# Six small moves in a three-layer transformer kernel bound by TensorE: casts, a weight's low half, a gelu table, gates, final gains and two convolution taps

## The reference

```python
def first_block(x, c, ctx, c_ctx, ...):            # DEPTH = 2 layers
    for l in range(DEPTH):
        with_ctx = l < DEPTH - 1                   # layer 0 also updates ctx
        u = x * (1.0 + sc1) + sh1                  # modulated by c; uc likewise
        y, yc = token_mixer(u, uc, rope, w_in[l], ...)
        x = layer_norm(alpha * x + g1 * y, ln1_g[l], ln1_b[l])
        x = layer_norm(alpha * x + g2 * sq_relu_mlp(x * (1.0 + sc2) + sh2, w1[l], ...), ...)

def token_mixer(...):
    a, qkv, o_pre, g_if, cq, ckv, kr, gates = split(u @ w_in + b_in)
    y_conv = conformer_conv(a, ...)       # h = val * sigmoid(gate); 31 taps by token; norm; product
    h_x = mlstm_bidir(q_x, k_x, v_x, ...) # chunks of 128 tokens, 4 heads, both directions
    o_x = mla_blockwise(...)              # low-rank queries and keys, 8 heads, softmax
    return gated_merge(gates, y_conv, y_ml, o_x @ w_mla_out, w_out, b_out)

def gated_merge(gates, y_a, y_b, y_c, w_out, b_out):
    g_a, g_b, g_c = split(sigmoid(gates))
    return (g_a * y_a + g_b * y_b + g_c * y_c) @ w_out + b_out
```

## Time and profile before

| | |
|---|---|
| median of 3 runs | 3194.83 us (3194.47 to 3195.56) |
| profiled execution, its own time | 3197.05 us |
| its span, first to last instruction | 3194.6 us |
| mean granted clock of TensorE | 0.997 |
| PE busy | 3147.1 us |
| DVE busy | 1995.1 us |
| ACT busy | 1223.0 us |
| POOL busy | 1207.0 us |

### The profile page before, as it was taken

How to read it: one execution, slowest core, us unless ns; L and a number is a source line. 1 busy time by engine, 2 the same in 40 slices (tenths; PEclk the granted TensorE clock), 3 DMA queues, 4 the chain that set the end, 5 groups by cost and what they waited for, 6 DMA issues and landing times. The chain is left out here.

```text
span 3194.6 us, 46651 instructions
## 1 busy us (share of the span) xinstructions
PE 3147.1 (99%) x17058; PEld 2549.9 (80%) x17058; DVE 1995.1 (62%) x2910; ACT 1223.0 (38%) x1744; POOL 1207.0 (38%) x610
## 2 busy tenths in 40 slices
PE   8999999999999999999999999999999999999998
PEld 7888557888888888887776477778988877788887
DVE  6958476448876423146997673678533676777626
ACT  3232345522244323133542555245333375322223
POOL 3332066233333232323441463544444324444443
PEclk9999999999999999999999999999999999999999
DMA  6222130235412222222222103663333232233333
GB/s 232 58 60 53 42 88 21 56 106 160 146 58 66 63 62 64 60 65 69 78 80 51 26 1 110 209 188 90 93 92 93 83 105 60 86 92 92 96 96 106
DMA packets 470029, 275.94 MB, mean 86 GB/s; under 512 B 53985, under 2 KB 453857, under 8 KB 468706
## 3 DMA queue, kind: packets, MB, share of 16 engines
q1 hardware_dynamic: 469714, 273.55, 29.1%
q10 hardware_dynamic: 144, 0.02, 0.0%
HBM read 269.31 MB, written 4.19 MB: 86 GB/s over the span
## 5 line engine op out<-in xcount | busy, mean ns | idle before, releaser
L386 POOL TENSOR_TENSOR weights_low<-weight_ring,weights_high 128x1024 fp32r<-128x1024 f32 (+1 forms) x399 | 970.5, 2434 | 1675.7 <-ACT weights_high L377 1660.6
L377 ACT ACTIVATE weights_high<-weight_ring 128x1024 fp32r<-128x1024 f32 (+1 forms) x408 | 410.2, 1006 | 1033.0 <-PE ps L487 991.9
L482 PE MATMUL ps<-features_high,weights_high 128*128 128x512 f32 (+2 forms) x1792 | 605.8, 353 | 4.2 <-DVE features_low L2904 2.4
L483 PE MATMUL ps<-features_low,weights_high 128*128 128x512 f32 (+2 forms) x1792 | 602.3, 353 | 0.0
L482 PEld LDWEIGHTS ps<-features_high,weights_high 128*128 128x128 f32 (+1 forms) x1792 | 336.9, 188 | 62.0 <-DVE features_low L3851 4.1
L483 PEld LDWEIGHTS ps<-features_low,weights_high 128*128 128x128 f32 (+1 forms) x1792 | 336.6, 188 | 51.6
L482 PE MATMUL ps<-u_high,weights_high 128*128 128x512 f32 (+2 forms) x944 | 364.7, 390 | 5.4 <-DVE u_low L4197 2.7
L487 PE MATMUL ps<-features_high,weights_low 128*128 128x512 f32 (+2 forms) x1792 | 365.9, 351 | 0.0
L483 PE MATMUL ps<-u_low,weights_high 128*128 128x512 f32 (+2 forms) x944 | 359.1, 385 | 0.0
L487 PEld LDWEIGHTS ps<-features_high,weights_low 128*128 128x128 f32 (+1 forms) x1792 | 288.9, 188 | 44.7
L1349 DVE SCALAR_TENSOR_TENSOR conv<-conv,vectors 128x512 f32<-128x512 f32 (+1 forms) x480 | 306.5, 708 | 1.2 <-DVE conv L1257 1.0
(11 more groups left out here) (665 smaller groups left out, 5290.2 us busy)
## 6 DMA issues: line engine op xcount, KB each, us to landing
weight_ring<-in_w SPq DMA_DIRECT2D x256, 256.0 KB, 3.0
weight_ring<-in_w_in SPq DMA_DIRECT2D x246, 256.0 KB, 3.2
conv<-in_w_mod_columns SPq DMA_DIRECT2D x64, 512.0 KB, 4.6
weight_ring<-in_w_up SPq DMA_DIRECT2D x88, 256.0 KB, 3.1
weight_ring<-in_w_out SPq DMA_DIRECT2D x48, 256.0 KB, 3.1
weight_ring<-in_w_mod SPq DMA_DIRECT2D x32, 256.0 KB, 3.5
weight_ring<-in_w_down SPq DMA_DIRECT2D x32, 256.0 KB, 3.0
first_modulation<-in_first_modulation SPq DMA_DIRECT2D x4, 1024.0 KB, 9.5
```

The costliest lines, as they stand in the source:

```text
L377: act.activation(core.ring_high[:, split_slot(run, q), 0:n], core.ring[:, slot, 0:n], ACT.Copy).then_inc(core.high_ready.sem, 1)
L386: pool.tensor_tensor(core.ring_low[:, split_slot(run, q), 0:n], core.ring[:, (run.first + q) % SLOTS, 0:n], high.bitcast(F32), ALU.subtrac ...
L482: pe.matmul(to, w_high[:, k, 0:m], high(k, a, b), start=(first and k == ks[0]), stop=False, skip_group_check=True)
L483: pe.matmul(to, w_high[:, k, 0:m], low(k, a, b), start=False, stop=False, skip_group_check=True)
```

## The change

Six places in the order of work, no new computation:

- Convolution of layer 1: `cuts` from (1, 11, 14, 17) to (1, 9, 12, 15). Two taps fewer stand before the first of the three later inputs, the distances between the inputs stay, two more taps follow the last.
- Layer 0's casts for the mLSTM stage move from behind step 1 to behind step 5, after the last turned key of the loop.
- Layer 1's first low half of the output weights is made by DVE inside the merge (after the first sum of the last pair) and no longer by POOL; POOL waits for all eight split tiles before it goes on with group 1.
- Mixer stage, DVE: gate 0's product stands ahead of the token scales, tiles 0 and 1 are split before gate 1's product.
- Mixer stage, ACT: an activation of one column loads gelu's table right after the square root; tile 0, gate 1 and tile 1 come before the second weight group's high half.
- Embedding stage, ACT: the final gains of tiles 4 and 5 stand before the last two sigmoids instead of behind them.

```diff
--- before.py
+++ after.py
@@ -1359,7 +1359,7 @@
                 nc.vector.tensor_scalar(conv[:, f, a:b], pads[:, f, at:at + b - a], w_dw[:, 0, f:f + 1],
                                         col(core, f"b_dw{l}", f), ALU.mult, ALU.add).then_inc(conv_step.sem, 1)
             if f == 0:
-                cuts = (1, 11, 21, CONV_K) if seam is None else (1, 11, 14, 17)
+                cuts = (1, 11, 21, CONV_K) if seam is None else (1, 9, 12, 15)
                 for q in range(1, 4):
                     taps(0, cuts[q - 1], cuts[q])
                     conv_input(q)
@@ -2231,7 +2231,7 @@
                     turning.clear_maxima()
                 if i in turn_at:
                     turning.copy_keys(dve, i - 1)
-                if i == turn_at[0]:
+                if i == (turn_at[-1] + 1 if both else turn_at[0]):
                     turning.round_triangles()
                     turning.round_ones(dve)
         dve.wait_ge(s["scored"].sem, s["scored"].at(2 * len(steps_of)))
@@ -2944,6 +2944,9 @@
                         nc.vector.tensor_tensor(m, m, prod[:, f, 0:w], ALU.add).then_inc(merged_step.sem, 1)
                         if (b, i) != (1, 3):
                             late.make(dve, b, i, f)
+                    if not both and last and b == 2 and f == 0:
+                        dve.wait_ge(core.split_ready.sem, split_count(run, 3, 3))
+                        low_part(core, dve, run_out, 0, 0)
                 if b == 0 and isinstance(i, int) and i == 0:
                     norm.scale(dve)
             if b == 0:
@@ -3570,7 +3573,12 @@
 
     @block.gpsimd
     def _(pool):
-        low_parts(core, pool, run_out, run)
+        if not both:
+            pool.wait_ge(merged_split.sem, merged_split.at(KT))
+            pool.wait_ge(core.split_ready.sem, split_count(run_out, 0, 0))
+        for g in range(0 if both else 1, run_out.groups):
+            low_part(core, pool, run_out, g // run_out.body, g % run_out.body)
+        low_parts(core, pool, run)
 
     @block.tensor
     def _(pe):
@@ -4186,6 +4194,12 @@
         nc.vector.tensor_tensor(mix[:, 0], misc, u[:, 0], ALU.mult).then_inc(gmlp_done.sem, 1)
         dve.wait_ge(mixed.sem, mixed.at(2))
         nc.vector.tensor_tensor(mix[:, 1], misc, u[:, 1], ALU.mult).then_inc(gmlp_done.sem, 1)
+
+        def gate_conv(f):
+            dve.wait_ge(gb_ready.sem, gb_ready.at(f + 1))
+            nc.vector.tensor_tensor(xc[:, f], xc[:, f], gb[:, f], ALU.mult).then_inc(xc_gated.sem, 1)
+
+        gate_conv(0)
         dve.wait_ge(std.sem, std.at(1))
         link(nc.vector.reciprocal(token_std, token_std))
         mark("token scales")
@@ -4197,12 +4211,9 @@
             nc.vector.tensor_tensor(split.low[:, k, :], mix[:, k], split.high[:, k, :].bitcast(F32), ALU.subtract)\
                 .then_inc(mix_split.sem, 1)
 
-        for k in (6, 7):
+        for k in (6, 7, 0, 1):
             split_mix(k)
-        for f in range(2):
-            dve.wait_ge(gb_ready.sem, gb_ready.at(f + 1))
-            nc.vector.tensor_tensor(xc[:, f], xc[:, f], gb[:, f], ALU.mult).then_inc(xc_gated.sem, 1)
-            split_mix(f)
+        gate_conv(1)
         for k in (2, 3):
             split_mix(k)
         dve.wait_ge(g_ready.sem, g_ready.at(2))
@@ -4587,13 +4598,14 @@
         high_part(core, act, run_out, 0, 0)
         act.wait_ge(sq_summed.sem, sq_summed.at(1))
         act.activation(token_std, token_sums, ACT.Sqrt, scale=1.0 / HD2, bias=core.eps[:, 1:2]).then_inc(std.sem, 1)
+        act.activation(core.eps[:, 3:4], core.eps[:, 0:1], ACT.Gelu_apprx_tanh)
         act.wait_ge(used.sem, group_done(core, run, 4, 1))
         for f in range(2):
             round_mix(6 + f, lambda: act.wait_ge(pooled_made.sem, pooled_made.at(f + 1)))
+        round_mix(0, lambda: act.wait_ge(gmlp_done.sem, gmlp_done.at(1)))
+        gate_conv(1)
+        round_mix(1, lambda: act.wait_ge(gmlp_done.sem, gmlp_done.at(2)))
         high_part(core, act, run_out, 0, 1)
-        for f in range(2):
-            round_mix(f, lambda: act.wait_ge(gmlp_done.sem, gmlp_done.at(f + 1)))
-        gate_conv(1)
         for f in range(2):
             round_mix(2 + f, lambda: act.wait_ge(xc_gated.sem, xc_gated.at(f + 1)))
         for f in range(2):
@@ -4922,12 +4934,15 @@
             act.activation(core.normed[:, k], x(k), ACT.Copy, scale=col(core, "final_g", k)).then_inc(final_gained.sem, 1)
 
         for i in range(KT // 2):
+            if i == KT // 2 - 1:
+                for f in range(2):
+                    final_gain(2 * (i - 1) + f)
             for f in range(2):
                 ahead(core, act, run, i // 2, 2 * (i % 2) + f, i >= 2)
                 act.wait_ge(free[f].sem, free[f].at(i + 2))
                 act.activation(sig[:, f], sig[:, f], ACT.Sigmoid).then_inc(gated.sem, 1)
             for f in range(2):
-                if i:
+                if 0 < i < KT // 2 - 1:
                     final_gain(2 * (i - 1) + f)
         act.wait_ge(totals.sem, totals.at(1 + 2 * late))
         for f in range(2):
```

## The result

The kernel became slower: 3202.91 us (median of 11 runs, 3200.54 to 3203.73) against 3194.83 (11 runs, 3191.89 to 3197.38), ratio 1.0025, 95% interval 1.0017 to 1.0033, that is +8 us with an interval of 5.4 to 10.5. The prediction had 3194.5 and a range up to 3199. The profiled execution took 3200.54 around a span of 3198.7; 4.1 of the 8 us are in its span, since this execution is the fastest of the eleven where the profiled one of before is 2.2 above its median. The profile's mean granted clock is 0.997, that of the ten other runs 0.995 to 0.996.

The account below looks back on a forecast made before the run. TensorE, busy 99% of the span, was taken as the bound. Terms 8.5 - 1.5 - 3.5 - 2.7 - 1.1 = -0.3 us gave 3194.5 on the median; 8-in-10 range 3185.5 to 3199.

Parts of the forecast that it names:

- A: Layer 1's convolution taps: first input 0.8 earlier, but TensorE idles 7.7 at the turned gate rows; +8.5 us.
- I charge one half clock stretch as behind the 2.4 us wait, 1.6: Within A, behind the 7.7 us idle time at the gate rows: one half clock stretch costing 1.6 us.
- the hold: Layer 1's last taps: GpSimd's three back-to-back instructions hold one VectorE tap until 1652.4, making TensorE +6.9 late.
- its bound of +10.1: Upper bound of A: half clock behind the gate-row wait twice as long as the profile rows show.
- Rival 1: Layer 1's last taps aren't held behind L1050; A = +0.5, sum -8.3, 3186.5 us, faster; chance 0.2.
- rival 3: Gate-row wait: half clock lasts longer in proportion to the wait, costing 5.3 instead of 1.6; 3198.2 us; chance 0.08.
- C: Layer 1, merge to output projection: VectorE's chain shortens, TensorE's wait falls from 2.45 to about 0.2; -3.5 us.
- -2.2 -1.7: Within C, at the merge's split tiles: 2.2 us less TensorE wait and 1.7 us less half clock.
- rival 2: A new wait over 2 us with half clock takes back gains: C + D = -2.5, 3198.2 us; chance 0.1.
- B: Layer 0's casts moved behind the last turned key's copy: TensorE's wait of 1.7 on turned keys shrinks; -1.5 us.
- D: Mixer to second output projection: waits 1.5 instead of 2.7, and the half clock stretch of 1.5 goes; -2.7 us.
- E: Tail: final gains before the last two sigmoids remove TensorE's wait of 0.9; -1.1 us.

## Why the prediction was wrong

**A, the step "I charge one half clock stretch as behind the 2.4 us wait, 1.6", failed; the hold did not.** The wait was 7.49 where 7.7 was forecast, at the instruction named, ended by L1267, with a tap held until the end of the second weight half. The run with one tap shows that it is a threshold (6.39 and +8.8 for half the edit), the run with GpSimd's halves moved that the halves make 4.7 of it. The half clock behind it lasted 7.1 us and cost 3.2 (table) to 3.5 (7.1 x 0.5), twice the charge: A = +9.3 (the run of the taps alone) to +9.7 (table) instead of +8.5. That is inside its bound of +10.1; the mechanism and the sign were right. Rival 1 (no hold) is out, rival 3 (longer half clock) half right: twice as long, not three times. Nor does the length follow the wait, as rival 3 had it: 7.0 us behind 2.79, 7.0 behind 6.39, 7.1 behind 7.49.

**C, the step "C = -3.5", failed, and this decides.** Its mechanism at the splits was right: no wait there, clock 1.0, -3.9 between the two traces. Its price, "-2.2 -1.7", was taken from one trace, which had the longest wait of seven and one of only two half clock stretches; the estimate from all seven is -2.1. Then I priced what is queued behind GpSimd's new wait and did not look at what that instruction, once it starts, lies against on VectorE. It holds the gated bias, eight numbers wide, on which ScalarE's 5 us stand with no slack: +3.9 in the trace after, 2.15 the wait (shown by the run with GpSimd behind the bias, where it is gone) and the rest mainly its half clock (which is there in two of the three traces with this wait, and missing without the taps: 2.14, clock 1.00). This is rival 2 by its effect, with 0.1 for its chance. The second cause was in none of the cases: two records more in VectorE's list, a gap of 0.35 us 400 us later, a hold, a wait of 1.36; four empty waits alone cost +4.0 (1 to 6.7 by the interval), and six took it away again. The estimate with all three is -2.1, +2.1 with 2/3 x 1.7 of half clock, and +1.4: +2.5. Alone C measured +2.6 (-0.6 to +5.1) where -3.5 was forecast: 6.1 of the 8.4 us between the forecast sum (-0.3) and the measured +8.1.

**B, D and E were right** in the one pair of traces in which they are told apart. B -1.7 for -1.5, D -3.3 for -2.7 with waits of 0.7 and less where 1.5 was forecast, E -1.2 for -1.1. D's half clock is no fixed sum either: with the mixer as before, behind the same wait of 2.33, the run with two empty waits has a clock of 1.00 over 3.8 us. The table load behind the square root took 1.28, beginning 0.02 behind the root's end, and the next instruction followed 0.01 later, much as in the earlier trace rows; the 2.66 of the Trainium skill (ScalarE: Activation LUTs, section "What ACT_TABLE_LOAD costs") doesn't show here:

```profile
2716.87 1.28 ACT L4601 ACT_TABLE_LOAD   x1
2718.16 0.20 ACT L4601 ACTIVATE eps<-eps 128x1 f32<-128x1 f32 x1
2718.53 1.67 ACT L4595 ACTIVATE u_high<-mixers 128x512 fp32r<-128x512 f32 x3 [0.16 <-PE ps L487]
```

**The sum.** +9.3 alone for the taps and -3.3 for all the rest make +6.0; measured +8.1, with 5.4 to 10.5 its interval. The 2 us between lie within that interval and aren't assigned.

**What stays open.** What fills the 0.35 us isn't shown: no record lies in the gap, and only that it goes with the place in the list is (there with two records more, not with none, one or five). Open too is why half clock comes behind the same wait in one execution and not in the next, and why the merge's wait varies from 0.91 to 2.45. The scatter of the timed runs goes with their granted clock: within the four empty waits' eleven runs it goes from 0.998 at 3194.4 us to 0.995 at 3203.12. So the difference of two profiled executions is not the difference of two medians: here +4.1 and +8.1.

## What to carry to other kernels

Before a start of one engine is moved, list what the other engine that shares its port has just then, down to instructions of eight numbers: a short one at the head of a long chain costs as much as a long one. Work between two fixed points has a cliff where it no longer fits before the neighbour's block: half the taps cost the same, so ask how far the last free instruction ended from that block, not how much is moved. And where one engine's instruction wins against a competitor's by a third of a microsecond, measure the kernel with a few empty instructions added too, or a gain and an accident can't be told apart. Before a wait's price goes into a sum, read it in several executions: one trace gave 3.9 us for a stretch that is worth 2.1 on average.

## What of the hardware was not expected

- A change of the length of an engine's instruction list by two records can move a time 400 us later: 0.41 us instead of 0.06 between the end of a semaphore wait and the next start, at the same instruction in all five kernels with two records more, and +4.0 us in the whole (four empty waits). One record more takes away a late start of 0.41 that the kernel before has 200 us earlier.
- GpSimd's tensor operation held VectorE's instructions on a few numbers as long as large ones: 2.17 for L2996 (8 columns) and 2.38 for L3374 (2 columns, a tensor_scalar) instead of 0.17. The Trainium skill (SBUF — State Buffer, section "SBUF: two separate sides") names two SBUF inputs or a two-port mode of VectorE as what contends; the first fits L2996, which of the two L3374 would be no run here tells.
- At a hand-over between two GpSimd instructions VectorE stayed out in the one-tap run too (one tap instruction across three of GpSimd's, 6.67 us).
- Half clock behind waits: 2.15 us of idle time, 0.66 over 4.5 us; 2.79, 0.51 over 7.0 us; 7.49, 0.50 over 7.1 us; and after 1.37 the same wait had 0.75 over 4.4 us in one trace and 1.00 in another:

```profile
2543.00:2547.40 4.40, 4.40 (x22) 3.63 (x23) 0.00 (x0) 1.44 (x3) 2.35 (x1) 0.75 0.02 4
```

```profile
2540.00:2544.40 4.40, 4.40 (x25) 3.56 (x26) 0.81 (x2) 0.36 (x1) 2.37 (x1) 1.00 0.01 4
```
